# Holding back GpSimd's low parts of one weight tile behind each of three norms

## The reference, cut to what matters

```python
# first block, before the feed-forward part
h = h + mix @ w_out
hn = rms_norm(h, ln2_w)
h = h + square(relu(hn @ w_up)) @ w_down
# second block: first norm
h = standardize(x) * (1.0 + sc1) + sh1
mix = hybrid_mixer(h, ...)
# second block: between mixer and feed-forward part
x = layer_norm(ALPHA * x + (1.0 + g1) * mix, ln1_gain, ln1_bias)
h = standardize(x) * (1.0 + sc2) + sh2
f = conv_glu_ffn(h, ...)
```

## Time and profile before

| what | us |
|---|---|
| median of 3 runs | 1534.7 (1532.49 to 1535.1) |
| the profiled execution's own time | 1526.97 |
| its span | 1525.2 |
| PE busy (matmul) | 1452.4, 95% of the span |
| DVE busy | 890.6, 58% |
| POOL busy | 684.0, 45% |
| ACT busy | 585.7, 38% |
| POOL's subtractions in the loop (L1513) | 440 of mean 1465 ns; idle before them 770.0, released by ACT |

### The profile page before, as it was taken

One profiled execution on the slowest core, in us unless ns is written; L12 is line 12 of the kernel. 1 busy time (PEld: TensorE's weight loads), 2 busy tenths in 40 slices (PEclk: granted clock), 3 DMA queues, 4 the chain that ended last, 5 costly groups with the idle time before them and its releaser, 6 DMA issues.

```text
span 1525.2 us, 19363 instructions
## 1 busy us (share of the span) xinstructions
PE 1452.4 (95%) x7136; PEld 1175.2 (77%) x7136; DVE 890.6 (58%) x1469; ACT 585.7 (38%) x838; POOL 684.0 (45%) x520
## 2 busy tenths in 40 slices
PE   4999999999999999998999999999988999999997
PEld 4777776678888787887888777778866888888886
DVE  4682657558867788886482546346675333332357
ACT  5332467544222122217342755544345331331231
POOL 2432145435655465553452424435532445344553
PEclk9999999999999999999999999999998999999999
DMA  7322130016746454232634533243213222223222
GB/s 290 106 83 104 56 111 2 29 44 217 253 171 227 157 193 167 83 111 97 146 131 137 184 111 131 104 179 125 97 56 138 83 102 94 102 89 111 83 83 83
DMA packets 48181, 185.70 MB, mean 122 GB/s; under 512 B 12960, under 2 KB 14112, under 8 KB 33248
## 3 DMA queue, kind: packets, MB, share of 16 engines
q1 hardware_dynamic: 30240, 165.53, 30.9%
q10 hardware_dynamic: 17856, 19.01, 4.4%
HBM read 169.71 MB, written 12.58 MB: 120 GB/s over the span
## 4 chain that ended last, share of the span: by engine, by line
issue 32%; PE 26%; POOL 24%; DVE 2%; ACT 0%; POOLq 0%; DVEq 0%
POOL wlo L1513 23%; PE bank L446 5%; PE bank L448 5%; PE bank L447 5%; PE bank L489 3%; PE bank L491 3%; PE bank L490 3%; PE bank L694 1%; DVE X L2402 0%; PE bank L470 0%; PE bank L765 0%; DVE X L2414 0%; POOL wlo L1521 0%; ACT FN L1023 0%; DVE st L1553 0%
## 5 line engine op out<-in xcount | busy, mean ns | idle before, releaser
L1513 POOL TENSOR_TENSOR wlo<-raw,whi 128x512 fp32r<-128x512 f32 x440 | 630.9, 1465 | 770.0 <-ACT whi L986 770.0
L446 PE MATMUL bank<-Ahi,whi 128*128 128x512 f32 x1088 | 434.9, 400 | 6.8 <-DVE X L1603 3.4
L447 PE MATMUL bank<-Alo,whi 128*128 128x512 f32 x1088 | 425.4, 391 | 0.0
L448 PE MATMUL bank<-Ahi,wlo 128*128 128x512 f32 x1088 | 425.3, 391 | 0.0
L986 ACT ACTIVATE whi<-raw 128x2048 fp32r<-128x2048 f32 x113 | 216.9, 1920 | 238.6 <-PE bank L491 197.6
L446 PEld LDWEIGHTS bank<-Ahi,whi 128*128 128x128 f32 x1088 | 205.5, 189 | 55.2 <-issue 4.8
L447 PEld LDWEIGHTS bank<-Alo,whi 128*128 128x128 f32 x1088 | 205.6, 189 | 43.8 <-issue 2.4
L448 PEld LDWEIGHTS bank<-Ahi,wlo 128*128 128x128 f32 x1088 | 205.3, 189 | 43.7
L489 PE MATMUL bank<-whi,Bhi 128*128 128x512 f32 x496 | 193.3, 390 | 1.7 <-DVEq L1880 1.7
L491 PE MATMUL bank<-whi,Blo 128*128 128x512 f32 x496 | 193.0, 389 | 0.0
L490 PE MATMUL bank<-wlo,Bhi 128*128 128x512 f32 x496 | 193.0, 389 | 0.0
(11 more groups left out here) (394 smaller groups left out, 1907.9 us busy)
## 6 DMA issues: line engine op xcount, KB each, us to landing
raw<-in_ws SPq DMA_DIRECT2D x113, 1024.0 KB, 5.0
adaw<-in_ada SPq DMA_DIRECT2D x48, 512.0 KB, 4.7
spill<-stage ACTq DMA_DIRECT2D x32, 256.0 KB, 2.3
X<-in_x SPq DMA_DIRECT2D x8, 512.0 KB, 5.9
gates<-spill SPq DMA_DIRECT2D x16, 256.0 KB, 5.4
w1k<-in_w1k SPq DMA_DIRECT2D x1, 2048.0 KB, 15.9
w1v<-in_w1v SPq DMA_DIRECT2D x1, 2048.0 KB, 20.1
XM<-spill ACTq DMA_DIRECT2D x8, 256.0 KB, 3.5
```

What stands on the lines that cost most here:

```text
L446: pe.matmul(ps[:], wh, hi[:, k], start=(k == 0), stop=False)
L447: pe.matmul(ps[:], wh, lo[:, k], start=False, stop=False)
L448: ins = pe.matmul(ps[:], wl, hi[:, k], start=False, stop=(k == kn - 1))
L1513: pool.tensor_tensor(wlo[slot][:, part], raw[slot][:, part], rd(whi[slot][:, part]), ALU.subtract).then_inc(sem("lo_split"), 1)
```

## The change

POOL's one long loop over tiles 14 to 111 is cut at three places. Before the low part of tiles 16, 48 and 80, POOL also waits for a semaphore of DVE: for `rstd_ready` at 8 (all four rows of norm 1), at 12 (of norm 2), and for `x_final` at 4 (all four rows of norm 3 have been written by `again`, the step before the last row's second scale). The tile after each of them (17, 49, 81) is then written out by hand, and loops run between. No computation changes, and no other engine's instructions.

```diff
@@ -1538,7 +1538,21 @@
                 gated(u)
             if n_ahead % 2:
                 low_part(n_ahead)
-            low_parts(n_ahead + n_ahead % 2, NTILES - NTILES % 2)
+            a = n_ahead + n_ahead % 2
+            for s, name in ((1, "wout.1.1"), (2, "dn3.1.1"), (3, "mix.1.1")):
+                t = last_tile(INDEX[name]) + 1
+                low_parts(a, t - t % 2)
+                if t % 2:
+                    low_part(t - 1)
+                if s < 3:
+                    pool.wait_ge(sem("rstd_ready"), NT * (s + 1))
+                else:
+                    pool.wait_ge(sem("x_final"), NT)
+                low_part(t)
+                if t % 2 == 0:
+                    low_part(t + 1)
+                a = t + 2 - t % 2
+            low_parts(a, NTILES - NTILES % 2)
             if NTILES % 2:
                 low_part(NTILES - 1)
```

## The result

| | before | changed |
|---|---|---|
| median of 5 runs each, us | 1532.49 (1529.89 to 1535.1) | 1541.18 (1539.81 to 1542.71) |
| profiled execution, own time, us | 1526.97 | 1542.71 |
| its span, us | 1525.2 | 1540.9 |

The changed kernel is slower: the ratio is 1.0059, with a 95% interval of 1.0042 to 1.0075, thus +9.0 us (6.4 to 11.5).

The account below looks back on a forecast made before the run. PE, busy 1452.4 of 1525.2 us, was taken as the bound, so only its standstills count. 3.7 + 3.0 - 1.5 + 1.1 = +6.3 us gave 1541.0 from a median of 1534.7; range 1535.5 to 1545.

Parts of the forecast that it names:

- Step 1: Row statistics of all three norms: without POOL beside them, DVE gains 0.2, 0.4 and 1.9 us.
- Step 2: Norm 1: POOL's four subtractions hold up four DVE operations, 3.9 us; PE's start +3.7, bounds 2.7 and 4.8.
- Step 3: Norm 2: again 3.9 us of hold-up, less 0.5 DVE idle time and 0.4 gained: +3.0, bounds 2.0 and 4.2.
- Step 4: Norm 3: 1.9 us gained, 0.4 given back at the last scale: -1.5, bounds -1.9 and 0.
- Step 5: Products behind norms 1 and 2: PE may start at its lower clock after standing still, +1.1 us, bounds 0 and 3.0.
- Step 6: POOL's next tile, the tile loads and the cut loops: enough slack, so no cost.
- A: Norms 1 and 2: DVE's parts are not held up, only 2.5 us gained, 1532.2; chance 0.12.
- B: Norms and later stages: delay is paid but half hidden by other waits, +1.8 us, 1536.5; chance 0.12.
- C: Norms 1 and 2: full collision and low clock twice, up to +12.0, typically +10 us, 1544.7; chance 0.12.
- D: All norms: the change does nothing because `hi_split` comes later than the new waits; chance none.

Follow-up runs that it names:

- second profile of the changed kernel: The changed kernel, unaltered, timed and profiled once more beside the kernel before: 1539.96 against 1531.31 us, ratio 1.0058.
- two kernels without that wait: Changed kernel without norm 3's wait (1.0071); kernel before with only two quarters of tiles 16 and 48 held back for the last scale (1.0048).
- with PE kept busy: Changed kernel plus matmuls with overwritten results ahead of transposes and of the products behind norms 1 and 2; two versions, 1.0049 and 1.0047 against the kernel before.

## Why the prediction was right, and which term was mis-sized

**Step 1, what is taken away: right.** From the last product matmul to the first part took 3.24 us in norm 1 and 4.15 in norm 2 before, 3.05 and 3.74 now: 0.19 and 0.41 gained, against 0.2 and 0.4. In norm 3 the last scale came 9.32 behind the last product matmul and now comes 7.43 behind it: 1.89, against 1.9.

**Step 2, norm 1: right.** Four stretched operations, 3.80, where 3.9 stood in the sum; the gap grew by 3.70, as predicted. The Trainium skill (SBUF — State Buffer, SBUF: two separate sides) would have it that the other engine is locked out for the whole instruction. By POOL's 1.26 that was the upper bound, 4.8; this trace shows 0.94 to 0.96 a piece, and the bound was not reached. The reason for the difference was not tested.

**Step 3, norm 2: right.** +2.81 against +3.0; 3.80 of stretch, less the idle time that covered 0.58 of it (four parts took 8.51 in place of 5.29), less 0.41.

**Step 4, norm 3: right in the gap, its worth not shown.** -1.47 against -1.5. The small rows of DVE:

```profile
1161.35 0.17 DVE L2443 RECIPROCAL sd<-sdx 128x1 f32<-128x1 f32 x1 [1.64 <-ACT sdx L1469]
1161.55 0.56 DVE L2445 TENSOR_TENSOR nmr<-tot,sd 128x1 f32<-128x1 f32 x1
1162.15 1.47 DVE L1598 CAST Ahi<-FN 128x512 fp32r<-128x512 f32 x1
1163.65 1.64 DVE L1600 TENSOR_TENSOR Alo<-FN,Ahi 128x512 fp32r<-128x512 f32 x1
1165.32 0.43 DVE L1598 CAST Ahi<-FN 128x512 fp32r<-128x512 f32 x1
```

The scale was stretched by 0.40, and the first part's two operations by 2.0, which ACT's pace covered by the fourth part. But the product then started at the low clock, and 1.64 was lost again against the profile before. The step had counted the gap alone. Against a kernel whose product starts at full clock the gain is gone by the middle of the product (long gaps of 22.11 and 22.04 against 22.03); where both start low, or both at full, it is 1.29 and 1.48. The timed kernels with norm 3's wait alone (0.9991 and 0.9998) neither show a gain of 1.5 us nor exclude it.

**Step 5, the clock: the term that was mis-sized.** It stood at 1.1, for norms 1 and 2 only, with bounds of 0 and 3.0. In the profile the three half products cost 1.74, 1.53 and 1.64 more: 4.9. The step had the right mechanism for norms 1 and 2 (3.3 there, just past its upper bound; the second profile of the changed kernel has 7.32 and 8.22, thus 3.9). It put nothing at norm 3, although its own row from 1144 to 1153 showed the low level right ahead of that product. Norm 3's 1.6 may not be an effect of the wait alone, since two kernels without that wait paid 1.5 there as well.

An estimate from the timed runs points the same way. On one chip, 25 runs of the kernel before have a mean granted clock of 0.9845 and a mean span of 1529.4, six of the changed kernel 0.9808 and 1538.0. One minus clock, times span, is 23.7 and 29.5, 5.8 apart; from run to run of the kernel before, the span grows by 0.68 to 0.82 us for each us of it (slopes fitted on the three chips), which makes 3.9 to 4.8. With the gaps' 5.0 that is 8.9 to 9.8, against 8.7 to 9.0 measured. This estimate takes in the low stretches of the whole program, and it assumes that the slope holds from one kernel to another. That is not shown: with PE kept busy this figure fell from 29.5 to 13.1 for the changed kernel, and its mean span by 2.4 us only.

**Step 6, what costs nothing: right.** POOL's next tile starts on ACT's signal at 354.03, 6.95 us after the moved one; ACT splits it at 352.04 without an idle row ahead of it. Its splits of later tiles at 363.12 and 374.00 show none either. In norm 2 POOL's next tile, at 720.52, stretched the eighth part too, which the step did not foresee; the part was done at 724.19, ahead of the second half's start at 725.35, so PE did not wait for it.

**Rivals.** A (not held up) is out by DVE's maxima of 1465 and 1661 ns. B (partly hidden) is out: the stretches behind norms 1 and 3 give back 0.33 and 0.04 us. C was right in that the clock stayed low more than once, wrong in the full collision; its total of +10 is nearer to the measured 9.0 than the forecast's 6.3 is. D is out by POOL's timeline. The range, 1535.5 to 1545, held the time, 1541.18, and the predicted 1541.0 itself is close partly by chance: it was built on a median of 1534.7, and five runs of the kernel before have 1532.49.

## What to carry to other kernels

Before moving work of GpSimd under work of VectorE, list the VectorE operations beside it by what they read. Here casts from SBUF to SBUF and operations with two inputs in SBUF paid one for one, 0.95 us for each 128x512 operation of POOL. Additions out of PSUM and the long row statistics paid nothing: in the kernel before, 18 such additions (L1603) and 19 BATCH_NORM_STATS2 (L1553) ran beside POOL's subtractions, and none took more than 0.70 us. So the same work cost only 0.2 and 0.4 where it was in norms 1 and 2, through one small operation each; in norm 3, beside the double norm's operations on SBUF, it cost 1.9.

Where TensorE stands still just ahead of a product, add the product's first microseconds at half clock to the price (1.5 to 1.7 us in each place in the profiled pair), and do not count a shorter standstill as a gain until the window behind it shows the clock, in more than one kernel. Check a shift at two marks, the start of the next product and its middle.

## What was not expected

The profile pair differs by 15.7 us, the medians by 8.7. 4.4 of it lies ahead of norm 1, where both kernels run the same code. The changed kernel's second profile has its last product matmul of norm 1 at 338.08, next to 337.72 in its first; the kernel before has 333.35. The low stretches fall at other points of the program, and why they do was not tested and stays open. It is a reason to count a shift within each norm, not from the program's start.

The steps of one element are held up as well: L2445, on 128x1, took 0.56 in place of 0.16 beside POOL, while RECIPROCAL on the same shape, just ahead of it, kept its 0.17. The first has two inputs in SBUF, the second one; this fits the list above, but no run here varied it.
